# Every tile on chip starts 32 bytes past a multiple of 128: a helper that fills each tensor's row

## The chip, the cores and the metric

The kernel runs on one core of one Trainium2 chip. The metric is device time of one execution, in microseconds, and lower is better.

## The reference, cut to what matters

The reference is one forward pass of three transformer-like blocks over a sequence of 512 positions with 1024 features, everything in float32. What fills the time is dense products of an activation with a weight matrix:

- block 1: a SwiGLU layer (1024 to 2816 and back), a mixer (attention in blocks of 128 keys beside a gated recurrence, two gated projections and an output projection), and a second SwiGLU layer;
- block 2: one wide projection into four mixers (a delta-rule recurrence, gated linear attention, an mLSTM and a state-space mixer), a gated merge, and a feed-forward layer with a causal convolution over three positions on both of its halves;
- block 3: a spatial gating mixer (1024 to 4096 and back), a forgetting attention, and two feed-forward layers (1024 to 2048) whose gate half alone has the convolution.

```python
def swiglu(x, w1, w3, w2):
    return (jax.nn.silu(x @ w1) * (x @ w3)) @ w2
...
def conv_gated_ffn(h, w_gate, w_up, conv_w, conv_b, w_down):
    a = h @ w_gate
    ...                       # causal convolution over 3 positions
    return (jax.nn.silu(a) * (h @ w_up)) @ w_down
```

## The kernel before, in words

**Layout.** Activations lie transposed: a tile `[128, k, 512]` holds feature `k*128 + partition` of all 512 positions. `x` is the residual, `xn` the normalised input of the next product, `hidden` the inner activation of a feed-forward layer.

**A product in three parts.** A float32 value is kept as a pair of rounded values, `hi` and `lo` (type fp32r). Each product of 128 input and 128 output features is three matmuls: (w_hi, x_hi), (w_hi, x_lo) and (w_lo, x_hi). The stationary operand is a slice of 128 columns (512 bytes of a partition's row) of the weight tile, the moving operand 512 columns (2048 bytes) of the activation. Each matmul has a weight load of its own, which the profile shows on a row called PEld. The lines are L280 (`Feed.products`, for the attention and the delta-rule stages), L1108 (`Flow.products`, for the stages named s1 to s4), L1916 (`Side.tensor`, for the stages named hg and br) and L1637, where the roles are turned: there a slice of `xn` is stationary and 512 columns of the weights move.

**How weights come.** SyncE loads a raw slice of 512 KB (128 partitions x 1024 floats), ScalarE rounds it into `w_hi` (L263, L1081, L1928), VectorE subtracts to get `w_lo` (L268, L1088, L1934), and TensorE makes 24 matmuls of it. Two or three slices are held in turn, 4096 bytes apart in a row.

**Stages.** The program is a sequence of blocks, each with its own tiles: s1 (first SwiGLU), att, hg (recurrence, with merge products beside it), s2 (merge, output, second SwiGLU), rw, br (three mixers of block 2 with projections beside them), s3 (merge, output, convolution feed-forward, spatial gating, feed-forward), fox (attention of block 3), s4 (its output and the last feed-forward). In s3 the feed-forward of block 2 has 22 tiles of 128 inner features, and each takes 48 matmuls and an epilogue of ScalarE and VectorE (`ConvGLU`: L1263, L1243, L1267, L1268, L1252, L1274, L1278 to L1280), in whose order the rounding of the next weights (L1081, L1088) is written as well. Each engine's order is written out by hand; engines meet by semaphores.

**Where the tiles lie.** Tiles are given places in a row of SBUF one behind the other as they are opened (an `ExitStack` closes them again), each rounded up to 32 bytes. The first, `table`, starts at byte 16512, a multiple of 128. `column` has 709 floats (2836 bytes, rounded 2848), so what stands behind it, `x`, `xn`, `rs` and the big tiles, starts at 32 modulo 128. All of these have rows that are multiples of 2048 bytes. Small tiles of a stage (`sink`, `gains`, `lbc`, a padded row of 514, 513 or 515 positions) shift the tiles behind them by 32, 64 or 96.

The moving operand of nearly all the dense matmuls starts at 416 modulo 512. The start of the stationary slice, and the distance from the start of the moving to the start of the stationary operand, both modulo 512, are worked out from the shapes:

| weights | stages | stationary modulo 512 | modulo 128 | distance modulo 512 |
|---|---|---|---|---|
| `s_w` in s1 and s2, `side` | s1, s2, hg, br | 416 | 32 | 0 |
| `s_w` in s3 and s4, `hg_w` | s3, s4, hg | 480 | 96 | 64 |
| `att_w` | att | 256 | 0 | 352 |
| `rw_w` | rw | 448 | 64 | 32 |
| `br_w` | br | 384 | 0 | 480 |
| `fox_w` | fox | 96 | 96 | 192 |
| L1637 (`xn` stationary, `s_w` moves) | s3 | 416 | 32 | 448 |

Of the kernel before, what the change touches and what calls it, by code (L numbers as in the profile page):

```python
# [1 line left out]


# [1 line left out]

# [1 line left out]

# [3 lines left out]
F32 = mybir.dt.float32  # L11
# [5 lines left out]
P = 128  # L17
# [77 lines left out]
COLUMN_WIDTH = _at  # L95


class Stage:


# [11 lines left out]
        return self.stack.__exit__(*e)  # L112

    def sb(self, name, shape, dtype=F32):
        return self.stack.enter_context(self.nc.sbuf_tensor(f"{self.name}_{name}", shape, dtype))

    def ps(self, name, shape):
        return self.stack.enter_context(self.nc.psum_tensor(f"{self.name}_{name}", shape, F32))
# [1709 lines left out]
class Sums:  # L1828


    def __init__(self, sb, rs):
        self.total, self.squares, self.sq = sb("total", [P, S]), sb("squares", [P, S]), sb("sq", [P, 2, S])
        self.rs, self.small = rs, sb("small", [P, S])
# [766 lines left out]
def branches(nc, c, a, xn, y_0, y_1, y_2, y_s, part, low, gates, inbox_a, inbox_b, more):  # L2600

    with Stage(nc, "br") as st:
        b = [st.ps(f"b{i}", [P, S]) for i in range(8)]
        side = Side(c, st, [b[6][:, :], b[7][:, :]], 4, more)
        achain, dchain = st.sem("achain"), st.sem("dchain")

        def place(name, make):
            with ExitStack() as s:  # L2610
                return make(lambda n, shape: s.enter_context(nc.sbuf_tensor(f"{name}_{n}", shape, F32)))
        box = [inbox_a[:, m * S:(m + 1) * S] for m in range(4)]
        pad_m = inbox_b[:, 0:2 * (S + 3)].rearrange("p (m t) -> p m t", m=2)
        box_m = [inbox_b[:, 2 * (S + 3) + m * S:2 * (S + 3) + (m + 1) * S] for m in range(2)]
        pad_s = inbox_a[:, 0:3 * (S + 3)].rearrange("p (m t) -> p m t", m=3)
        box_s = inbox_a[:, 3 * (S + 3):3 * (S + 3) + S]
        lanes = Lanes(st, c, low, st.sb, place)
        gla = place("gla", lambda sb: Gla(side, "gla", low[:, 0, :], y_1, sb, box))
        ml = place("ml", lambda sb: Mlstm(side, lanes, "ml", low[:, 0, :], y_2, sb, pad_m, box_m))
        sd = place("sd", lambda sb: Ssd(side, lanes, "sd", low[:, 0, :], y_s, sb, pad_s, box_s))  # L2620
        lanes.scratch(inbox_b[:, 0:3 * S].rearrange("p (n t) -> p n t", n=3), part[:, 0:2, :], part[:, 2, :])
        st.sb("held", [P, 17 * S])
        side.allocate()
        ins = {gla: (a["gla_w"], box), ml: (a["ml_w"], [pad_m[:, 0, 3:], pad_m[:, 1, 3:], *box_m]),
               sd: (a["sd_w"], [pad_s[:, 0, 3:], box_s, pad_s[:, 1, 3:], pad_s[:, 2, 3:]])}
        order = [(branch, h) for branch in (gla, ml, sd) for h in range(4)]
        gla.ask(xn, a["gla_w"][0], box)
        first = len(side.pieces)
        given = {(sd, 0): [0], (sd, 1): [1], (sd, 2): [2], (sd, 3): [3, 4, 5]}
        for n, (branch, h) in enumerate(order):  # L2630


            at = len(side.pieces)
            nth, y = {gla: (0, y_0), ml: (1, y_1), sd: (2, y_2)}[branch]
            if n + 1 < len(order):
                nxt, nh = order[n + 1]
                w_d, outs = ins[nxt]
                nxt.ask(xn, w_d[nh], outs)
            for t in given.get((branch, h), []):
                side.sigmoid(xn, a["mg2_w"][t, 3, :, 0:D], gates[t])  # L2640
            side.gated(xn, y, 4, [(t, a["mg2_w"][t, nth]) for t in (2 * h, 2 * h + 1)], part, part if nth else None)
            branch.beside.append((at, len(side.pieces)))

        with nc.Block() as block:
            @block.sync
            def _(sp):
                gla.sync(sp, a["gla_fup"])
                side.sync(sp)

            @block.tensor  # L2650
            def _(pe):
                lanes.tensor_move(pe, b)
                side.tensor(pe, first * DT)
                lanes.tensor_turn(pe, b)
                lanes.tensor_ends(pe, b)
                gla.tensor(pe, b)
                ml.tensor(pe, b)
                sd.tensor(pe, b)

            @block.scalar  # L2660
            def _(act):
                q = InOrder(act, achain)
                side.scalar_first(act)
                side.scalar(act, 1)
                lanes.scalar(act, q, b)
                side.scalar(act, first - 1)
                gla.scalar(act, q, b)
                ml.scalar(act, q, b, gla)
                sd.scalar(act, q, b)

            @block.vector
            def _(dve):
                q = InOrder(dve, dchain)
                side.vector_first(dve)
                gla.zero(dve)
                side.vector(dve, q, 1)
                lanes.vector(dve, q)
                side.vector(dve, q, first - 1)
                lanes.vector_columns(dve, q, b)
                lanes.vector_decays(dve, q, b)  # L2680
                q(dve.memset(pad_m[:, :, 0:3], 0.0))
                gla.vector(dve, q, b, ml)
                q(dve.memset(pad_s[:, :, 0:3], 0.0))
                ml.vector(dve, q, b, sd)
                sd.vector(dve, q, b)
# [383 lines left out]
def build(nc, a, out_d):  # L3069

    with ExitStack() as keep:
        def sb(name, shape, stack=keep):
            return stack.enter_context(nc.sbuf_tensor(name, shape, F32))

        def pair(name, tiles_, stack):
            return Pair(lambda n, shape, dtype: stack.enter_context(nc.sbuf_tensor(n, shape, dtype)), name, [P, tiles_, S])

        table, column = sb("table", [P, TABLE_WIDTH]), sb("column", [P, COLUMN_WIDTH])

        with ExitStack() as s:  # L3080
            more = [s.enter_context(nc.sbuf_tensor(f"side_{n}", [P, 2, D], F32R)) for n in ("hi", "lo")]
        x, kept = sb("x", [P, DT, S]), nc.dram_tensor("kept", (P, DT, S), F32).ap()
        c = Ctx(nc, table, column)

        with ExitStack() as blocks:
            xn, rs = pair("xn", DT, blocks), sb("rs", [P, S], blocks)

            with ExitStack() as s:
# [221 lines left out]
```

How the kernel before makes its waits and increments, by code:

```python
    def __call__(self, ins):  # L131
        ins.then_inc(self.sem, 1)
        self.n += 1
        self.eng.wait_ge(self.sem, self.base + self.n)
# [14 lines left out]
    def wait(self, eng, name, r=0):  # L149
        eng.wait_ge(self.sem, r * len(self.names) + self.names.index(name) + 1)
# [1 line left out]
    def wait_round(self, eng, r):  # L152
        eng.wait_ge(self.sem, r * len(self.names))
# [75 lines left out]
    def wait(self, eng, k):  # L230
        if self.ready:
            sem, base, step = self.ready
            eng.wait_ge(sem, base + step * (k + 1))
# [17 lines left out]
    def load(self, sp, r, m, first, source):  # L251
        s, slot = self.at(r, m)
        if not first or m >= self.slots:
            sp.wait_ge(self.parted, s - self.slots + 1)
        cols = source.shape[-1]
        sp.dma_start(self.raw[:, slot, 0:cols], source).then_inc(self.landed[slot], 16)
# [1 line left out]
    def round(self, act, r, m, first, cols):  # L258
        s, slot = self.at(r, m)
        act.wait_ge(self.landed[slot], (r * (self.per // self.slots) + m // self.slots + 1) * 16)
        if not first or m >= self.slots:
            act.wait_ge(self.used, s - self.slots + 1)
        act.activation(self.hi[:, slot, 0:cols], self.raw[:, slot, 0:cols], ACT.Copy).then_inc(self.rounded, 1)
# [1 line left out]
    def rest(self, dve, r, m, cols):  # L265
        s, slot = self.at(r, m)
        dve.wait_ge(self.rounded, s + 1)
        dve.tensor_tensor(self.lo[:, slot, 0:cols], self.raw[:, slot, 0:cols], self.hi_value[:, slot, 0:cols],
                          ALU.subtract).then_inc(self.parted, 1)
```

## Time and profile before

| | us |
|---|---|
| median of 3 runs | 4438.67 (4435.94 to 4443.2) |
| the profiled execution, its own time | 4443.0 |
| its span in the trace | 4441.2 |
| TensorE busy | 4021.4 (91%), 18490 matmuls |
| weight loads busy | 3245.4 (73%) |
| VectorE, ScalarE busy | 2139.9 (48%), 1520.6 (34%) |
| granted TensorE clock | 0.955 of full |

Busy time of an engine is the union of its instructions' intervals. Matmuls overlap in the trace (one is shown 390 to 400 ns long while the next starts after some 230), so their mean length is not what one costs: the step from one start to the next is, and it is read from start times, or as busy time over count in a stretch without a gap.

### The profile page before, as it was taken

To read this page: it belongs to the slowest core of one execution; us is meant where nothing else is said; L and a number is where in the kernel's file an instruction comes from. 1 tells how busy PE (TensorE), PEld (TensorE's weight loads), DVE (VectorE), ACT (ScalarE), POOL (GpSimd) and SP (SyncE) were. 2 spreads that over 40 slices of the span, in tenths; PEclk is the share of its full clock that TensorE was granted. 3 is DMA by queue.
4 is the path that set the end of the run, shared out by engine and by line. 5 is a ranking of instruction groups with operands and counts; after the bars stand their busy time and mean duration, and the time that the engine had idled before them with its cause. 6 is when DMAs were issued, how large, how long until landed. Compare 5 with 4: busy or idle time off the path is not lost. (4 is left out here: it accounts for less than half of the span.)

```text
span 4441.2 us, 46915 instructions
## 1 busy us (share of the span) xinstructions
PE 4021.4 (91%) x18490; PEld 3245.4 (73%) x18490; DVE 2139.9 (48%) x3342; ACT 1520.6 (34%) x2330; POOL 0.2 (0%) x4
## 2 busy tenths in 40 slices
PE   9997769998899778877999998999998998887998
PEld 7885658887788667776767776777787886666886
DVE  3334564444533445554445556665346564233563
ACT  2223444443322322224444443333322322444322
POOL 0000000000000000000000000000000000000000
PEclk9998989999999889989999999999998999899999
DMA  4231112222223210102222223233332332110332
GB/s 145 95 97 55 34 43 90 76 81 95 85 96 95 62 37 17 35 1 78 72 67 69 74 69 102 85 88 96 93 104 62 90 96 67 56 43 28 100 95 81
DMA packets 94321, 328.08 MB, mean 74 GB/s; under 512 B 10416, under 2 KB 11440, under 8 KB 93744
## 3 DMA queue, kind: packets, MB, share of 16 engines
q1 hardware_dynamic: 94128, 325.40, 23.6%
q8 instruction: 134, 2.20, 0.2%
q14 instruction: 59, 0.48, 0.0%
HBM read 319.06 MB, written 6.29 MB: 73 GB/s over the span
## 5 line engine op out<-in xcount | busy, mean ns | idle before, releaser
L1088 DVE TENSOR_TENSOR s_w_lo<-s_w_raw,s_w_hi 128x1024 fp32r<-128x1024 f32 (+2 forms) x394 | 471.8, 1198 | 652.3 <-ACT s_w_hi L1081 649.5
L1108 PE MATMUL s_acc<-xn_hi,s_w_hi 128*128 128x512 f32 x1744 | 695.0, 398 | 46.3 <-DVE s_w_lo L1088 18.7
L1108 PE MATMUL s_acc<-xn_lo,s_w_hi 128*128 128x512 f32 x1744 | 689.5, 395 | 0.0
L1108 PE MATMUL s_acc<-xn_hi,s_w_lo 128*128 128x512 f32 x1744 | 688.9, 395 | 0.0
L1081 ACT ACTIVATE s_w_hi<-s_w_raw 128x1024 fp32r<-128x1024 f32 (+2 forms) x394 | 405.5, 1029 | 556.7 <-PE s_acc L1108 442.2
L1108 PEld LDWEIGHTS s_acc<-xn_hi,s_w_hi 128*128 128x128 f32 x1744 | 330.3, 189 | 134.7 <-DVE s_w_lo L1088 26.5
L1108 PEld LDWEIGHTS s_acc<-xn_hi,s_w_lo 128*128 128x128 f32 x1744 | 330.4, 189 | 75.5
L1108 PEld LDWEIGHTS s_acc<-xn_lo,s_w_hi 128*128 128x128 f32 x1744 | 330.6, 190 | 74.8 <-issue 1.2
L1108 PE MATMUL s_acc<-hidden_hi,s_w_hi 128*128 128x512 f32 x784 | 308.0, 393 | 0.7 <-DVE s_w_lo L1088 0.7
L1108 PE MATMUL s_acc<-hidden_lo,s_w_hi 128*128 128x512 f32 x784 | 308.0, 393 | 0.0
L1108 PE MATMUL s_acc<-hidden_hi,s_w_lo 128*128 128x512 f32 x784 | 308.0, 393 | 0.0
L1108 PEld LDWEIGHTS s_acc<-hidden_hi,s_w_hi 128*128 128x128 f32 x784 | 147.4, 188 | 34.2 <-DVE s_w_lo L1088 1.1
L1108 PEld LDWEIGHTS s_acc<-hidden_lo,s_w_hi 128*128 128x128 f32 x784 | 147.4, 188 | 33.3
L1108 PEld LDWEIGHTS s_acc<-hidden_hi,s_w_lo 128*128 128x128 f32 x784 | 147.4, 188 | 33.1
L1916 PE MATMUL br_b<-xn_hi,side_hi 128*128 128x512 f32 x368 | 152.3, 414 | 5.5 <-DVE side_lo L1934 5.5
L1916 PE MATMUL br_b<-xn_hi,side_lo 128*128 128x512 f32 x368 | 144.7, 393 | 0.0
L1916 PE MATMUL br_b<-xn_lo,side_hi 128*128 128x512 f32 x368 | 144.7, 393 | 0.0
L1243 ACT ACTIVATE gate<-pad,column 128x512 f32<-128x512 f32 x54 | 44.1, 817 | 261.9 <-DVE pad L1263 261.9
L1916 PE MATMUL hg_b<-xn_hi,side_hi 128*128 128x512 f32 x256 | 104.8, 409 | 16.6 <-DVE side_lo L1934 10.2
L1916 PE MATMUL br_b<-xn_hi,br_w_hi 128*128 128x512 f32 x256 | 105.6, 412 | 9.5 <-ACT inbox_a L1953 6.8
L1219 DVE SCALAR_TENSOR_TENSOR gate<-gate,s_acc 128x512 f32<-128x512 f32 x44 | 30.3, 689 | 153.1 <-ACT gate L1214 153.1
L1934 DVE TENSOR_TENSOR side_lo<-br_w_raw,side_hi 128x1024 fp32r<-128x1024 f32 (+1 forms) x52 | 60.1, 1162 | 89.4 <-ACT side_hi L1928 89.3
(669 smaller groups left out, 7531.3 us busy)
## 6 DMA issues: line engine op xcount, KB each, us to landing
s_w_raw<-in_f_up SPq DMA_DIRECT2D x132, 512.0 KB, 3.8
s_w_raw<-in_g_up SPq DMA_DIRECT2D x64, 512.0 KB, 3.7
s_w_raw<-in_f_down SPq DMA_DIRECT2D x48, 512.0 KB, 3.5
hg_w_raw<-in_hg_w SPq DMA_DIRECT2D x32, 512.0 KB, 4.1
s_w_raw<-in_g_down SPq DMA_DIRECT2D x32, 512.0 KB, 3.8
br_w_raw<-in_mg_w SPq DMA_DIRECT2D x30, 512.0 KB, 3.6
fox_w_raw<-in_fox_w SPq DMA_DIRECT2D x27, 512.0 KB, 3.6
hg_w_raw<-in_mg_w SPq DMA_DIRECT2D x24, 512.0 KB, 3.8
```

Of the source, the lines that this page charges most:

```text
L1081: act.activation(self.hi[:, s % self.SLOTS, 0:cols], self.raw[:, s % self.RAW, 0:cols], ACT.Copy).then_inc(self.rounded, 1)
L1088: dve.tensor_tensor(self.lo[:, s % self.SLOTS, 0:cols], self.raw[:, s % self.RAW, 0:cols], self.hi_value[:, s % self.SLOTS, 0:cols], ALU.s ...
L1108: last = pe.matmul(out, w[:, slot, tile_cols(k)], v[:, p.k0 + k, :], start=p.start and k == 0 and n == 0, stop=p.stop and k == p.kt - 1 an ...
L1219: q(dve.scalar_tensor_tensor(prod, prod, 0.5, self.acc(t, 1), ALU.mult, ALU.mult))
L1243: act.activation(out[:, i, :], self.pad[:, 2 * i + side, 0:S], ACT.Identity, scale=w(0, t), bias=b(t)).then_inc(self.tapped, 1)
L1916: last = pe.matmul(out, w[slot][:, tile_cols(k)], v[:, k, :], start=k == 0 and n == 0, stop=k == kt - 1 and n == 2)
L1934: dve.tensor_tensor(self.lo[s % self.SLOTS][:, 0:cols], self.raw[:, s % self.RAW, 0:cols], self.hi[s % self.SLOTS][:, 0:cols].bitcast(F32) ...
```

## The change

A helper `room` opens a tile and, behind it, a fill tensor that takes the rest of its row up to a multiple of 128 bytes. All places where the kernel opens small or odd tiles go through it. In front of everything 8 floats (32 bytes) are taken, so that every tile starts at 32 modulo 128. Nothing reads or writes the fill tensors; no instruction is added, removed or moved.

```diff
+LINE = 128
+
+
+def room(nc, stack, name, shape, dtype):
+
+    t = stack.enter_context(nc.sbuf_tensor(name, shape, dtype))
+    fill = -((4 * math.prod(shape[1:]) + 31) // 32 * 32) % LINE // 4
+    if fill:
+        stack.enter_context(nc.sbuf_tensor(f"{name}_fill", [P, fill], dtype))
+    return t
...
     def sb(self, name, shape, dtype=F32):
-        return self.stack.enter_context(self.nc.sbuf_tensor(f"{self.name}_{name}", shape, dtype))
+        return room(self.nc, self.stack, f"{self.name}_{name}", shape, dtype)
...
-                return make(lambda n, shape: s.enter_context(nc.sbuf_tensor(f"{name}_{n}", shape, F32)))
+                return make(lambda n, shape: room(nc, s, f"{name}_{n}", shape, F32))
...
         def sb(name, shape, stack=keep):
-            return stack.enter_context(nc.sbuf_tensor(name, shape, F32))
+            return room(nc, stack, name, shape, F32)
...
+        keep.enter_context(nc.sbuf_tensor("first_fill", [P, 8], F32))
         table, column = sb("table", [P, TABLE_WIDTH]), sb("column", [P, COLUMN_WIDTH])
```

With it the distance from the moving to the stationary operand, modulo 512, is again worked out from the shapes, counted in units of 128 bytes behind `xn`. In s3 and s4 a padded tile of 65 units and `gains` of 1 unit stand before the weights among tiles of whole multiples of 512 bytes: 66 units, so 256. It is 256 in att, hg, br and fox too, and for L1637; 61 units give 128 in rw; it stays 0 in s1, in s2 and for `side`. `table` moves from 0 to 32 modulo 128, the small tiles of rw from 64, those of gla, ml and sd (stage br) from 0, to 32.

## Rows read from the trace of the kernel before

**Rows 1.** The page: busy us of each engine (share of the span), count of instructions.

```profile
PE 4021.4 (91%) x18490; PEld 3245.4 (73%) x18490; DVE 2139.9 (48%) x3342; ACT 1520.6 (34%) x2330; POOL 0.2 (0%) x4
```

**Rows 2.** Windows: us, then busy (count) of PE, PEld, DVE, ACT, POOL; clock, DMA.

```profile
100.00:300.00 200.00, 200.00 (x884) 165.65 (x883) 75.97 (x90) 47.54 (x55) 0.00 (x0) 1.00 0.31 95
3450.00:3650.00 200.00, 200.00 (x858) 160.83 (x857) 117.95 (x151) 63.27 (x76) 0.00 (x0) 1.00 0.31 95
4200.00:4400.00 200.00, 200.00 (x859) 161.32 (x858) 107.90 (x135) 56.07 (x66) 0.00 (x0) 1.00 0.32 95
```

**Rows 3.** Timeline of PE in br (start us, us, instruction): 47, then 48 matmuls.

```profile
2591.28 0.39 PE L1916 MATMUL br_b<-xn_lo,br_w_hi 128*128 128x512 f32 x1
...
2602.00 0.39 PE L1916 MATMUL br_b<-xn_hi,br_w_lo 128*128 128x512 f32 x1
2602.22 0.39 PE L1916 MATMUL br_b<-xn_hi,side_hi 128*128 128x512 f32 x1
...
2612.88 0.40 PE L1916 MATMUL br_b<-xn_hi,side_lo 128*128 128x512 f32 x1
```

**Rows 4.** Timeline of PE: 63 matmuls of fox; 287 of L1637.

```profile
3782.94 0.40 PE L280 MATMUL fox_pj<-xn_hi,fox_w_hi 128*128 128x512 f32 x1
...
3797.14 0.40 PE L280 MATMUL fox_pj<-xn_hi,fox_w_lo 128*128 128x512 f32 x1
3277.88 0.39 PE L1637 MATMUL s_acc<-s_w_hi,xn_lo 128*128 128x512 f32 x1
...
3343.35 0.40 PE L1637 MATMUL s_acc<-s_w_lo,xn_hi 128*128 128x512 f32 x1
```

**Rows 5.** Line L268 on VectorE: ns min/median/max, starts, forms.

```profile
L268 DVE TENSOR_TENSOR fox_w_lo<-fox_w_raw,fox_w_hi x27: 1217/1226/1226, 3777.7 to 4084.1; 128x1024 fp32r<-128x1024 f32 x27
L268 DVE TENSOR_TENSOR att_w_lo<-att_w_raw,att_w_hi x18: 1216/1226/1226, 399.5 to 627.6; 128x1024 fp32r<-128x1024 f32 x18
L268 DVE TENSOR_TENSOR rw_w_lo<-rw_w_raw,rw_w_hi x13: 1215/1217/1226, 1572.1 to 1908.2; 128x1024 fp32r<-128x1024 f32 x13
```

**Rows 6.** Groups by form of PE: count, busy us, mean ns, idle before.

```profile
L746 PE MATMUL rw_b<-low,rw_up 128*128 128x512 f32 x24 | 10.9, 592 | 0.0
L419 PE MATMUL att_sc<-att_box,table 128*128 128x512 f32 x24 | 11.0, 593 | 0.0
L2146 PE MATMUL br_b<-gla_v,gla_kt 128*128 128x128 f32 x56 | 6.9, 275 | 0.0
L2146 PE MATMUL hg_b<-hg_v,hg_kt 128*128 128x128 f32 x112 | 13.8, 275 | 0.0
```

**Rows 7.** Windows of L1108 alone, from s3 to the end, and its 22 tiles.

```profile
2690.00:4441.00 1751.00, 1234.40 (x5208) 981.59 (x5206) 0.97 0.27 81
2785.00:3044.00 259.00, 248.58 (x1049) 195.82 (x1047) 1.00 0.29 85
```

**Rows 8.** Waits: PE from 2850 to 3050, DVE from 2800 to 3040.

```profile
PE s_acc L1108 <- DVE s_w_lo L1088: 10.4, 16, 0.7
DVE s_w_lo L1088 <- ACT s_w_hi L1081: 73.3, 40, 1.8
```

**Rows 9.** Waits of DVE from 3490 to 3650.

```profile
DVE pad L1263 <- PE s_acc L1108: 17.0, 14, 1.3
```

**Rows 10.** Timeline of DVE: the same instruction, one tile later.

```profile
2906.75 0.68 DVE L1263 TENSOR_TENSOR pad<-s_acc,rs 128x512 f32<-128x512 f32 x1
...
2918.88 0.68 DVE L1263 TENSOR_TENSOR pad<-s_acc,rs 128x512 f32<-128x512 f32 x1
```

**Rows 11.** Windows of the tiles hg_w_lo and br_w_lo.

```profile
655.00:1040.00 385.00, 56.94 (x144) 27.06 (x144) 22.02 (x18) 0.98 0.25 77
2015.00:2690.00 675.00, 131.24 (x328) 62.66 (x328) 51.49 (x50) 0.96 0.23 72
```

**Rows 12.** Windows of L280: att and fox.

```profile
395.00:655.00 260.00, 106.13 (x384) 73.29 (x384) 0.90 0.14 44
3770.00:4105.00 335.00, 148.48 (x576) 105.92 (x576) 0.91 0.15 44
```

More of the change, by code:

```diff
@@ L4 @@
 from contextlib import ExitStack
+import math
 import numpy as np
```

## The prediction

> **What bounds the kernel now.** I read the page first. TensorE is busy 91% of the span, VectorE and ScalarE under half [rows 1]; the granted clock is 0.955 of full over the span. (Its weight loads, at 73%, run beside the matmuls.) So the question is not who waits but what one dense matmul costs, and where TensorE is really the bound. In what follows a pace is the time from one matmul's start to the next.
>
> The view by windows answers the first. In a stretch that TensorE fills without a gap, busy time over count is the pace. In s1, from 100 to 300 us, 884 matmuls overlap the 200 us, about two of them cut by the edges: 200/882 is 226.7 ns. The same shape of matmul on the same line in s3 and s4 gives 858 and 859, less one or two for the edges: 200/857 is 233.4 ns [rows 2]. The clock is 1.00 in all three, the DMA share the same. So a late stage pays some 6.7 ns more for each matmul.
>
> The timeline of TensorE in br shows that the stage is not the cause. 47 matmuls with weights from `br_w` go from 2591.28 to 2602.00, 10.72/46 = 233.0 ns each; the next instruction takes its weights from `side`, and 48 of those go from 2602.22 to 2612.88, 10.66/47 = 226.8 ns each [rows 3]. Line, shape, moving operand and bank are the same; the weight tile alone differs. What differs in the tile is where it starts. I take the start addresses of the section on the kernel and set paces beside the distance from moving to stationary operand, modulo 512: distance 0 (s1, `side`) has 226.7; 64 (s3, s4) 233.4; 480 (`br_w`) 233.0; 192 (fox) 14.20/62 = 229.0; and 448 (L1637) 65.47/286 = 228.9 [rows 2 to 4].
>
> That list says two things. First, 32 modulo 128 for a start is not by itself the quantity: L1637's stationary slice starts at 32 modulo 128 and it is not at 226.7, and `fox_w` and s3's weights both start at 96 modulo 128, against the same moving start, with paces of 229.0 and 233.4. So the distance counts, and with a period longer than 128. Second, 192 and 448 are 256 apart and have one pace to 0.1 ns, with opposite roles. I take that for a period of 256: pace is a function of the distance modulo 256.
>
> **The change, part by part.** It adds no instruction, no wait and no transfer; it moves tiles. After it the distance is 256 modulo 512 in att, hg, br, s3, s4 and fox and for L1637, which is 0 modulo 256: by the rule above these paces become 226.7. In rw it becomes 128, a distance of which no row tells; its cost is bounded by the paces seen, 226.7 to 234, against 233 now.
>
> Term 1, the s stages. Line L1108 has 5208 matmuls from 2690 us on [rows 7]. At 233.3 less 226.7, that is 6.67 ns, they are worth 34.7 us if TensorE is the bound everywhere. It is not. In the feed-forward of block 2 (22 tiles, 48 matmuls each, 1056 in all; 1049 fall in the stretch shown [rows 7]) TensorE waits 16 times for 0.65 us on the low part of the weights, while VectorE in the same stretch waits for ScalarE's rounding alone, 73.3 us in 40 waits, and never for TensorE [rows 8]. Two occurrences of L1263 lie 12.13 us apart [rows 10], and 48 matmuls at 233.3 ns take 11.20. So the tile's time is that of a closed ring of VectorE and ScalarE (pad, tap, round, rest, two taps, twice, and the epilogue), with TensorE inside it: faster matmuls only lengthen its waits, from 0.9 to 1.25 us a tile. Those 1056 matmuls are worth nothing (7.0 us off). In the later feed-forward layers, where only one half has the convolution, VectorE does wait for TensorE, 14 times for 1.2 us at the first of its waits in a tile [rows 9]; a tile gets 48 x 6.67 ns = 0.32 us shorter, well inside 1.2, so TensorE stays the bound. Left: 4152 x 6.67 ns = 27.7 us.
>
> Term 2, L1637: 384 matmuls, 228.9 to 226.7, 0.9 us.
>
> Term 3, hg and br: 3 x 144 = 432 matmuls with weights from `hg_w` and 3 x 328 = 984 from `br_w` [rows 11]. 1416 x 6.67 ns = 9.4 us. TensorE fills nearly all of these stages, but recurrences run beside the products; I count 85% of it, 8.0 us, and keep 5 to 11 for the range (a few matmuls at a switch between the two weight tiles are slow now as well).
>
> Term 4, att and fox: 384 and 576 matmuls [rows 12]. For fox 2.3 ns each is 1.3 us. For att I have no run in the rows; with s3's 6.67 ns it is 2.6 us. The softmax chain holds TensorE up in much of both, so half: 2.0 us, bounds 0.5 and 4. rw: 288 matmuls beside chains of VectorE, an unknown distance: taken at nothing, bounds -1 and +2 us.
>
> Edits at nothing. VectorE's weight subtraction has a median of 1226 ns with its tiles at 96 and at 0 modulo 128, and 1217 at 64 [rows 5]: no engine but TensorE shows an address. Plain float32 matmuls of 512 columns have the same mean with both operands at 32 modulo 128 (592) as with one at 32 and `table` at 0 (593), and those of 128 columns 275 ns with tiles at 0 and at 32 [rows 6]. So the move of `table` and of the small tiles is free; from below and above I allow 1 us. What hides it, if ScalarE or VectorE should change by some 10 ns at an instruction, is their idle half; only the ring of the 22 tiles would show it, 22 x 4 x 10 ns = 0.9 us.
>
> Sum: 27.7 + 0.9 + 8.0 + 2.0 = 38.6 us off the profiled execution's 4443.0, that is 4404.4. Its time is 4.3 above the median of the runs; off the median of 4438.7 the forecast is 4400. Its own range: 34 to 45 us off with 3 us of measurement, 4391 to 4408.
>
> **A rule against it.** Rows 3 show two weight tiles, one moving operand and two paces. The Trainium skill, in "SBUF — State Buffer", section "Who interferes with whom", gives TensorE two read ports of its own, one for the moving operand and one for weight loads, independent of each other, and says that it never waits on anyone; then the distance of the two starts could cost nothing, and the sum would be zero. By that rule the time would stay at 4438.7, which is rival B; the trace disagrees with 233.0 against 226.8 ns within 22 us of each other.
>
> **The rivals.**
>
> A. The period is 512 or more, and distance 256 is not like 0. For it: every fast row has distance 0 modulo 512, and I have no row at 256. Against: the one pace of 192 and 448. If 256 runs like 192 does, at 229.0, the s stages give 4152 x 4.33 = 18.0, hg and br 1416 x 4.33 x 0.85 = 5.2, att 0.8: 24 off, 4415. If it runs at 233.3 as 64 does, only L1637 and fox change, both a little slower (384 x 4.4 and half of 576 x 4.3 ns, 2.9 us): 4442, no change to be told.
>
> B. No effect of the distance; paces belong to the weight tile for another reason (its writer, its place far up in the row); the change does then not do what it says, 4438.7. `s_w` of s1 lies in the same part of the row as that of s3 and has the same writer, so 2 in 100.
>
> C. The other side: distance 256 brings the two reads together more than any distance now. One mechanism, in each dense matmul, slower than before from a pace of 233.3 up. The step seen between good and bad is 6.67 ns; one more of it, 240.0, costs 27.7 in s, 384 x 11.1 ns = 4.3 at L1637, 8.0 in hg and br, half of 576 x 11 ns = 3.2 in fox and 1 in att: 44 us, 4483. The ring of the 22 tiles would hide it there still (48 x 240 ns = 11.5 of 12.13 us). Against: the equality of 192 and 448.
>
> D. The VectorE and ScalarE ring takes over in the two later feed-forward layers too, 2 x 16 x 48 = 1536 matmuls, 10.2 us less: 4410. Against: VectorE's waits for TensorE there are four times what a tile loses.
>
> **How the numbers follow.** Forecast (4400): 78 in 100. D (4410): 8. A with a part of the gain (4415): 5. A without gain (4442) and B (4438.7): 4 and 2. C (4483): 3. 0.2% is 9 us, about what can be told from no change here. Faster: 78 + 8 + 5 = 91. Same: 6. Slower: 3. The range reaches below the forecast's own for the case that hg, br and the attentions give all they have (52 us at most with rw and the switches, and 1 us of error: 4386), above to D: 4387 to 4413 leaves out A, B, C and some of the ends.
>
> **What would show it.** In the changed kernel's trace, busy over count in full stretches of s3 and s4 must be 226.7 ns as in s1, and 882 matmuls must fit 200 us; `br_w` and `side` must have one pace; L1637 and fox must fall to 226.7 as well. The 22 tiles must keep 12.13 us each, with TensorE's waits in them grown to some 1.25 us. If s3 stays at 233 and L1637 leaves 228.9, the period is longer than 256 (A); if the 22 tiles get shorter, my ring is wrong; if rw's pace moves, that gives the value at 128. Most dangerous to the forecast is the period, which rests on two rows.

## The result and the profile after

The changed kernel takes 4409.93 us (median of 4 runs, 4401.99 to 4413.45) beside 4439.49 for the kernel before on the same chip: ratio 0.9928 [0.9913, 0.9943], 29.6 us off. On another chip it took 4407.33 (5 runs) beside 4439.71, ratio 0.9927 [0.9914, 0.9941], 32.4 us off. The profiled execution is the lowest of the first four, 4401.99 us, against the profiled 4443.0 of before: 41.0 us. Forecast 4400, range 4387 to 4413: the medians lie inside it, on the upper side.

The page of the changed kernel, busy us of each engine. TensorE has 48.1 us less than in [rows 1] for the same 18490 matmuls and its weight loads 5.8 us less; VectorE and ScalarE have not moved by 2 us.

```profile
PE 3973.3 (90%) x18490; PEld 3239.6 (74%) x18490; DVE 2138.1 (49%) x3342; ACT 1520.7 (35%) x2330; POOL 0.2 (0%) x4
```

Windows of the changed kernel, columns as in [rows 2]: s1, then s3, then s4.

```profile
100.00:300.00 200.00, 200.00 (x884) 165.62 (x883) 75.40 (x90) 47.05 (x55) 0.00 (x0) 1.00 0.30 95
3450.00:3650.00 200.00, 200.00 (x882) 165.22 (x882) 121.69 (x156) 64.85 (x77) 0.00 (x0) 1.00 0.31 95
4150.00:4350.00 200.00, 200.00 (x884) 165.58 (x883) 114.35 (x144) 58.50 (x69) 0.00 (x0) 1.00 0.32 98
```

Where s3 and s4 had 858 and 859 matmuls in 200 us they now have 882 and 884, as s1: one pace, 226.7 ns. The timeline of TensorE in br, the stretch of [rows 3]: 48 matmuls with weights from `br_w` (the first one starts with a longer load) and then 48 from `side`.

```profile
2578.80 0.48 PE L1930 MATMUL br_b<-xn_hi,br_w_hi 128*128 128x512 f32 x1
...
2589.57 0.39 PE L1930 MATMUL br_b<-xn_hi,br_w_lo 128*128 128x512 f32 x1
2589.80 0.39 PE L1930 MATMUL br_b<-xn_hi,side_hi 128*128 128x512 f32 x1
...
2600.45 0.39 PE L1930 MATMUL br_b<-xn_hi,side_lo 128*128 128x512 f32 x1
```

10.77/47 = 229.1 ns with that first start in it (the passes of br that start without one have 226.7), and 10.65/47 = 226.6 for `side`. The step between the two tiles of [rows 3] is gone. The same view for L1651 (L1637 before) and rw, against [rows 4]:

```profile
3257.73 0.39 PE L1651 MATMUL s_acc<-s_w_hi,xn_lo 128*128 128x512 f32 x1
...
3322.60 0.39 PE L1651 MATMUL s_acc<-s_w_lo,xn_hi 128*128 128x512 f32 x1
1697.27 0.80 PE L294 MATMUL rw_b<-xn_hi,rw_w_hi 128*128 128x512 f32 x1
...
1703.01 0.40 PE L294 MATMUL rw_b<-xn_hi,rw_w_lo 128*128 128x512 f32 x1
```

L1651: 64.87/286 = 226.8 ns, 228.9 before. rw, the one stage left at a distance of 128, has 232.3 ns over the gap-free intervals of its passes: the value that no row of before held. (The first of the lines shown is long; from the second, at 1697.90, to the last it is 5.11/22 = 232.3.)

The 22 tiles of block 2's feed-forward: the timeline of VectorE, every second occurrence of L1277 (L1263 before), and the waits of TensorE and of VectorE there, against [rows 8, 10]. (Columns of waits: us in total, times, longest.)

```profile
2893.06 0.68 DVE L1277 TENSOR_TENSOR pad<-s_acc,rs 128x512 f32<-128x512 f32 x1
...
2905.19 0.68 DVE L1277 TENSOR_TENSOR pad<-s_acc,rs 128x512 f32<-128x512 f32 x1
```

```profile
PE s_acc L1122 <- DVE s_w_lo L1102: 15.1, 16, 1.0
```

```profile
DVE s_w_lo L1102 <- ACT s_w_hi L1095: 67.8, 37, 1.8
```

12.13 us a tile, as before. TensorE's wait has gone from 0.65 to 0.94 us, 16 times; VectorE waits for ScalarE alone. From the first of the 44 occurrences to the last it is 259.93 us before and 259.85 now, so what these matmuls gained was waited away again. In the later feed-forward (VectorE's waits, 3460 to 3600 us, against [rows 9]) VectorE still waits for TensorE, so TensorE is the bound there:

```profile
DVE pad L1277 <- PE s_acc L1122: 10.4, 11, 1.0
```

### The profile page after: what moved, and what is told of

It is laid out like the page before. It is cut to its first block and busy times, and to the rows that moved or that the text cites. A ratio compares the mean times of both kernels' runs of the same rounds, so it can differ in the third digit from the quotient of the medians.

```text
span 4400.1 us, 46915 instructions
## 1 busy us (share of the span) xinstructions
PE 3973.3 (90%) x18490; PEld 3239.6 (74%) x18490; DVE 2138.1 (49%) x3342; ACT 1520.7 (35%) x2330; POOL 0.2 (0%) x4
```

## The experiments

Twelve runs (the last is the changed kernel again), in four groups, each group on one chip with its own runs of the kernel before (medians 4440.95, 4439.71, 4438.84 and 4439.27). "Distance" is from the start of the moving to that of the stationary operand, modulo 256. Stages are followed through the profiles from their first matmul to the first of the next.

### Is it the distance, and what is its period?

**map_distances** and **map_distances_2**: the changed kernel, with empty bytes taken before the rounded weights of some stages.

```diff
+SHIFT = {"s1": 96, "s2": 160, "s3": 32, "s4": 64, "att": 128, "hg": 160, "br": 192, "rw": 32, "fox": 480}   # map_distances
+SHIFT = {"s1": 192, "s2": 32, "s3": 128, "s4": 224}                                                       # map_distances_2
+def shift(st):
+    n = SHIFT.get(st.name, 0) // 4
+    if n:
+        st.stack.enter_context(st.nc.sbuf_tensor(f"{st.name}_shift", [P, n], F32))
...
+        shift(st)
         self.hi, self.lo = st.sb("w_hi", [P, slots, cols], F32R), st.sb("w_lo", [P, slots, cols], F32R)
```

> The changed kernel with a block of empty bytes in front of the rounded weights of each stage, so that each stage has another distance from moving to stationary operand. Distances modulo 512 are then 96 in s1, 160 in s2, 288 in s3, 320 in s4, 384 in att, 416 for hg_w, 448 for br_w, 160 in rw, 224 in fox; side and the order of work stay. My theory (pace is a function of the distance modulo 256): s3 runs as rw did before at 32, 233.4 ns; s4 as s3 did before at 64, 233.3; att as rw of the changed kernel at 128, some 232.2; br_w as fox did before at 192, 229.0; fox as br_w did before at 480, 233.3; s1 as att did before at 352, 234.3; rw, s2 and hg_w (160, 160, 416) have one pace of their own between 229 and 235. Rival (period 512 or more): these pairs, 256 apart, have nothing in common, and at least two of s3, s4, br_w and fox miss those paces by more than 1 ns. Rival (period 128): s1 at 96 and fox at 224 run alike, s2 at 160 like s3 at 288, hg_w at 416 too, and rw at 160. Whole time by my theory: 12 us more in s1, some 13 in s2, 28 in s3 and s4, 10 in the rest: about 4465 to 4475.

> The changed kernel with empty bytes before the rounded weights of four stages, other distances than in the first map, each one that another stage has shown: s1 at 192, s2 at 32, s3 at 128, s4 at 224. If the pace belongs to the distance and not to the stage: s1 229.0 ns (as br and fox at 192), s2 233.3 (as rw at 32 before), s3 232.3 (as att and rw at 128), s4 233.4 (as br before and fox at 224). If it belongs to the stage, s1 and s2, which read 234.3 and 233.3 in the first map, come out some other way. 4455 to 4465 us.

4469.51 us and 4452.16 us, one run each (the second below what was expected, 4455 to 4465). Windows of TensorE, the first kernel and then the second: us, busy (count), clock, DMA. In each kernel the four stretches are s1, s2, s3, s4.

```profile
100.00:300.00 200.00, 200.00 (x855) 1.00 0.30 93
1200.00:1400.00 200.00, 200.00 (x859) 1.00 0.29 95
3500.00:3650.00 150.00, 150.00 (x643) 1.00 0.30 93
4190.00:4340.00 150.00, 150.00 (x645) 1.00 0.31 94
```

```profile
100.00:300.00 200.00, 200.00 (x875) 1.00 0.30 95
1200.00:1400.00 200.00, 200.00 (x858) 1.00 0.29 94
3500.00:3650.00 150.00, 150.00 (x647) 1.00 0.31 95
4190.00:4340.00 150.00, 150.00 (x645) 1.00 0.31 95
```

The stage s1, at 884 in the changed kernel, has 855 at 96 and 875 at 192: the stage does not make the pace. Mean interval between starts, over the gap-free runs of matmuls in all traces (L1660 is L1637 in the two map kernels):

| distance modulo 256 | ns | read in |
|---|---|---|
| 0 | 226.7 | all stages |
| 32 | 233.3 | s3, s2; rw before 233.0 |
| 64 | 233.3 | s3 and s4 before, s4 |
| 96 | 234.3 | s1; att before 234.2 |
| 128 | 232.4 | att, rw, s3, L1660 |
| 160 | 233.3 | s2, rw, hg |
| 192 | 228.9, or 233.3 | s1, most of br; L1637 before has both, fox before one or the other by profile |
| 224 | 233.3 | fox, s4, L1660; br before 233.0 |

Except at 192, all stages at one distance agree to some 0.4 ns, and so do the distances that lie 256 apart (0 and 256, 32 and 288, 64 and 320, 96 and 352, 128 and 384, 160 and 416, 224 and 480). The period is 256; rival A and rival C (256 worse than before) are out. The sharp part is that 0 alone is free: the seven other steps of 32 bytes cost 2.2 to 7.6 ns a matmul.

At 192 there are two paces, and the kernel before has both. [rows 4] show the last 287 of L1637's 384 matmuls. The 96 ahead of them, with operands in the same tiles, go at 22.17/95 = 233.4 ns; sixteen small matmuls and one of L1637 lie between:

```profile
3253.46 0.40 PE L1637 MATMUL s_acc<-s_w_hi,xn_hi 128*128 128x512 f32 x1
...
3275.63 0.40 PE L1637 MATMUL s_acc<-s_w_lo,xn_hi 128*128 128x512 f32 x1
3275.86 1.95 PE L1721 MATMUL s_stat<-pad,table 128*128 128x128 f32 x16
```

All four profiles in which this line is at 448 show it so. fox at 192 has 229.0 over the 63 matmuls of [rows 4]; in before_round_first, where fox's tiles lie in the same places, the same stretch has 14.23/61 = 233.3:

```profile
3766.32 0.40 PE L280 MATMUL fox_pj<-xn_lo,fox_w_hi 128*128 128x512 f32 x1
...
3780.55 0.39 PE L280 MATMUL fox_pj<-xn_hi,fox_w_lo 128*128 128x512 f32 x1
```

What picks the pace at 192 stays open. At 0 all 82 gap-free runs of 100 matmuls or more, in ten profiles, have 226.7 to 226.8.

**start_at_0**: the changed kernel without the first 32 bytes.

```diff
-        keep.enter_context(nc.sbuf_tensor("first_fill", [P, 8], F32))
```

> The changed kernel without the 32 bytes that stand first: every tile starts at 0 modulo 128 in place of 32, and every distance between tiles stays. My theory (the distance of the two starts alone counts): 226.7 ns in every stage as in the changed kernel, the time the same within 0.2%, about 4408, ratio to the kernel before 0.993. Rival (the place itself counts, 32 modulo 128 being the good one): dense matmuls in all stages at 229 to 234 ns, 9200 in the s stages alone, so 4440 to 4480, slower than the kernel before.

4402.75 us (5 runs, 4402.46 to 4406.33), ratio 0.9916 [0.9903, 0.993]; all paces stay at 226.7, rw at 232.4. That everything begins at 32 modulo 128 does nothing to the paces (the time is 5 to 7 us below the changed kernel's two medians, which are of other chips); what the change does is to fill the rows, and with that to bring the distances to 0. Rival B's other causes (place in the row, writer of the tile) fall with it and with the maps.

**fine_distances** and **fine_distances_2**: the changed kernel; the weights are read some bytes further on in their tile.

```diff
+def weights(st, name, slots, cols):
+    n = SHIFT.get(st.name, 0) // 4      # s1 4, s2 16, s3 8, s4 252 bytes; in the second s1 16, s2 4, s3 252, s4 8
+    t = st.sb(name, [P, slots * cols + 64], F32R)
+    return t[:, n:n + slots * cols].rearrange("p (s c) -> p s c", s=slots)
```

> The changed kernel with the rounded weights moved by less than 32 bytes inside their tiles: distances modulo 256 of 4 in s1, 16 in s2, 8 in s3 and 252 (4 short of 256) in s4, 0 elsewhere but in rw. If two streams of reads meet in units of some tens of bytes, a shift of 4 or 8 changes nothing (226.7 ns in s1, s3, s4) and 16 little. If the good pace belongs to the exact distance, these run near the 233.3 of 32. I lean to the first at 4, 8 and 252 and expect 226.7 to 230 at 16; whole time then 4405 to 4415, by the rival about 4440 to 4460.

> The changed kernel with the rounded weights read from some bytes further on inside their tile, the four values of the first fine run handed to other stages: s1 16, s2 4, s3 252, s4 8 bytes. In the first run the pace at a fixed distance of 16 (s2) and of 252 (s4) was 233.33 in one gap-free run of matmuls and 226.67 in the next, that at 8 (s3) 230.7 throughout but for L1651's 233.3, that at 4 (s1) 232.4. If a fine distance leaves the matmuls two or more paces between which a gap chooses: s1 (16) and s3 (252) show 226.7 and 233.3 in turns, s2 (4) and s4 (8) something between. If pace is a plain function of distance, also below 32 bytes, s1 reads one value throughout. 4415 to 4445 us.

4438.47 and 4459.06 us, one run each (the second above the 4415 to 4445 expected). My lean, that a few bytes cost nothing, was wrong: 4 bytes cost 5.7 ns (232.4 in s1 and in s2), 8 bytes 4.0 (230.7 in s3 and in s4), 16 bytes 6.7 where they cost. But the pace is no plain function here. The timeline of s2 in the first of the two (16 bytes), around a wait of 1.06 us:

```profile
1179.88 0.39 PE L1129 MATMUL s_acc<-xn_hi,s_w_lo 128*128 128x512 f32 x1
1180.12 0.40 PE L1129 MATMUL s_acc<-xn_hi,s_w_hi 128*128 128x512 f32 x1
1180.35 0.39 PE L1129 MATMUL s_acc<-xn_lo,s_w_hi 128*128 128x512 f32 x1
1180.58 0.40 PE L1129 MATMUL s_acc<-xn_hi,s_w_lo 128*128 128x512 f32 x1
1182.04 0.50 PE L1129 MATMUL s_acc<-xn_hi,s_w_hi 128*128 128x512 f32 x1 [1.06 <-DVE s_w_lo L1109]
1182.38 0.39 PE L1129 MATMUL s_acc<-xn_lo,s_w_hi 128*128 128x512 f32 x1
1182.60 0.39 PE L1129 MATMUL s_acc<-xn_hi,s_w_lo 128*128 128x512 f32 x1
1182.83 0.39 PE L1129 MATMUL s_acc<-xn_hi,s_w_hi 128*128 128x512 f32 x1
```

Windows of TensorE around it, in the same kernel:

```profile
1090.00:1140.00 50.00, 50.00 (x216) 1.00 0.30 101
1190.00:1390.00 200.00, 200.00 (x884) 1.00 0.30 99
```

The 59 matmuls ahead of the wait go at 233.3 ns, the 1511 behind it at 226.7, with operands in the same places. In the second kernel s1, at 16 as well, has 233.3 throughout. At 252 the first kernel's s4 has 226.7 and, behind a gap, 233.3; the second's s3 has 233.3 but for a few short runs, one of them a tile of 48 between two waits (from 2942.6 us, 226.7). L1658 (L1637 before), where the roles are turned, is at 248 in the first kernel and has 233.3; it is at 4 in the second and has 226.7, where s1 and s2 at 4 have 232.4. So there are two paces for at least 4, 16 and 252, as for 192 above, and a stage can change from one to the other at a wait. What picks it stays open.

### What are the terms worth, one by one?

In all three the kernel before is filled in part: `room` fills only the tiles named.

```diff
-    if fill:
+    if fill and name.startswith(WIDE):
+WIDE = ("pad3", "gains3", "pad4", "gains4")                                      # scratch_only
+WIDE = ("hg_", "br_", "gla_", "ml_", "sd_", "inbox_a", "inbox_b")                # branches_only
+WIDE = ("att_", "fox_")                                                          # attention_only
-        keep.enter_context(nc.sbuf_tensor("first_fill", [P, 8], F32))
```

> The kernel before, with only the tiles pad and gains of Scratch (stages s3 and s4) filled up to 128 bytes: it takes the s3 and s4 stages and the 287 matmuls of L1637 to the distance 0 modulo 256 and leaves hg, br, att, rw and fox where they were. My theory: terms 1 and 2 of the prediction alone, 28.6 us of the 38.6, so 4440 - 28.6 = 4411 us (4409 to 4415). The rival that the gain lies in the fill of all tiles (their starts modulo 128, VectorE's and ScalarE's accesses too) expects at most half of the whole, 4425 or more.

> The kernel before, with only the tiles of the stages hg and br (with gla, ml, sd and the two inboxes of br) filled up to 128 bytes: both rounded weights come to distance 0 modulo 256 and nothing else moves. Term 3 of the prediction alone: 8.0 us (5 to 11), so 4440 - 8 = 4432 us, with hg_w and br_w at 226.7 ns instead of 233.3 and 233.0. The run scratch_only measured 4412.95 against 4439.71 and the whole change 4407.33, so terms 3 and 4 together may be worth 5.6 us only; by that this run would read 4434 to 4436. A rival by which hg and br are set by the lanes beside the matmuls expects 4439 to 4441.

> The kernel before, with only the tiles of the two attention stages (att and fox) filled up to 128 bytes, which brings both rounded weights to distance 0 modulo 256. Term 4 of the prediction alone: 2.0 us (0.5 to 4), 4438 against 4440 us. What is open: in the five profiles with att at distance 0 its stage, from its first matmul to the first of the next stage, took 259.8 to 264.5 us (mean 261.0), in the four at 96 it took 264.5 to 265.7 (mean 265.3), which would be 4.3 us and this run 4435.5; fox showed nothing (331.1 against 330.0). The sum of parts says 32.4 - 26.8 - 2.8 = 2.8 us for it, 4437. A stage time of 264 or more here would make the 4.3 us chance.

The pages of scratch_only and of branches_only, busy time:

```profile
PE 3984.4 (90%) x18490; PEld 3243.0 (74%) x18490; DVE 2139.7 (49%) x3342; ACT 1520.3 (34%) x2330; POOL 0.2 (0%) x4
```

```profile
PE 4014.8 (90%) x18490; PEld 3244.7 (73%) x18490; DVE 2139.2 (48%) x3342; ACT 1520.8 (34%) x2330; POOL 0.2 (0%) x4
```

scratch_only: 4412.95 us (5 runs), ratio 0.9941 [0.9928, 0.9955], 26.8 us off where 28.6 were predicted. TensorE's busy time fell by 37.0 and the profiled execution by 32.9 (4443.0 to 4410.15); in the 22 tiles its waits rose from 10.4 to 16.2 us. Two small tiles a stage, in s3 and s4, make five sixths of the whole change's 32.4 us.

branches_only: 4436.02 us (11 runs), ratio 0.9993 [0.9984, 1.0002], 2.8 us off (7 off to 1 on) where 8.0 were predicted. The long gap-free runs of `hg_w` and `br_w` are at 226.7, and TensorE's busy time is 6.6 us less, but the time is not. The lengths of the stages, in the ten profiles other than those of the map and fine kernels (us; for s3 those with the rounding moved, below, are left out):

| stage | distance not 0 | distance 0 |
|---|---|---|
| s3 | 1088.2 to 1089.5 (3 profiles) | 1069.6 to 1071.2 (4) |
| s4 | 331.6 to 333.3 (4) | 322.6 to 323.9 (6) |
| hg | 383.0 to 385.5, mean 384.2 (4) | 380.8 to 383.3, mean 381.8 (6) |
| br | 669.9 to 675.3, mean 672.2 (4) | 669.7 to 673.5, mean 670.6 (6) |
| att | 264.5 to 265.7 (4) | 259.8 to 264.5 (6) |
| fox | 328.6 to 331.7 (4) | 329.7 to 331.6 (6) |

s3 and s4 give 27 us, and their two columns do not overlap. hg gives most of its 2.9 us (432 matmuls), br a fourth of its 6.6 (984), and one stage's profiles differ by as much. br has waits for ScalarE's and VectorE's steps of the recurrences; that the missing part goes there is likely, and no run shows it.

attention_only: 4441.28 us (11 runs, 4431.95 to 4448.43), ratio 1.0007 [0.9998, 1.0016]: no gain to be told, 2.0 us on (1 off to 7 on). Yet its profile shows the att stage at 260.1 us, as four of the five others with att at distance 0 in the table (259.8 to 260.5; one had 264.5), where the four with att at 96 had 264.5 to 265.7. (In map_distances_2 and the two fine kernels, also at 0, it took 264.3, 261.1 and 268.1.) Windows of 401 to 640 us, before, then attention_only, then the changed kernel on the second chip:

```profile
401.00:640.00 239.00, 189.23 (x912) 151.28 (x912) 127.89 (x405) 90.73 (x270) 0.00 (x0) 0.91 0.14 44
```

```profile
401.00:640.00 239.00, 188.56 (x947) 152.17 (x945) 131.46 (x426) 94.64 (x284) 0.00 (x0) 0.93 0.14 44
```

```profile
401.00:640.00 239.00, 188.94 (x924) 152.40 (x923) 128.88 (x411) 91.49 (x273) 0.00 (x0) 0.91 0.14 44
```

The granted clock of the stretch is 0.93 in the shorter one and 0.91 in the two longer ones, of which the second has att at 0 as well; so most of the 4 us of a profile goes with the clock, not with the pace. Over a whole run the same shows: the runs of attention_only at a mean clock of 0.954 took 4439 to 4448 us, those at 0.956 and 0.957 took 4432 to 4436. Whether the distance has a part in that clock is open; the runs leave it a gain of 1 us at most.

### Is the ring what holds the 22 tiles?

ScalarE's rounding of the next weights goes ahead of its tap or Silu in `ConvGLU.scalar`. **round_first** is the changed kernel with it, **before_round_first** the kernel before with it.

```diff
+            self.flow.round(act, s + self.flow.SLOTS)
             if p.bank == 0:
                 self.tap(act, t, 0)
             else:
                 act.wait_ge(self.convolved, t + 1)
                 act.activation(gate, gate, ACT.Silu).then_inc(self.gated, 1)
                 if len(self.taps) > 1:
                     self.tap(act, t, 1)
-            self.flow.round(act, s + self.flow.SLOTS)
```

> The changed kernel with one change of order: in the epilogue of the convolution feed-forward ScalarE rounds the next weights before it makes the first tap, not after it. It tests the claim that the 22 tiles of the feed-forward of block 2 are bound by a closed ring of VectorE and ScalarE (12.13 us a tile with either layout). My theory: VectorE's two waits of 1.83 us a tile for the rounding shrink to some 0.4, the ring falls to about 9.5 us, and TensorE becomes the bound with 48 x 226.7 ns = 10.88 us a tile: 1.25 us x 22 = 27 us off, about 4381. Rival (TensorE or the loads of weights are the bound there in another way): the tiles stay within 0.3 us of 12.13 and the time within 7 us of the changed kernel's.

> The kernel before with the one move of the run round_first (ScalarE rounds the next weights ahead of its tap or Silu in ConvGLU), and no fills: the s stages of block 2 keep their distance of 64 and 233.3 ns a matmul. My theory: the ring of VectorE and ScalarE is what set 12.13 us a tile in the first FFN of block 2, in the kernel before as in the changed one. With the ring shortened the tiles there go by the matmuls, 48 x 233.3 ns = 11.20 us, so 17 to 22 tiles win 0.93 us each: 16 to 20 us, a time of 4420 to 4425 us. Then the distance is worth more once the ring is gone: round_first against this run should be 4423 - 4387 = 36 us, against the 30 us of the changed kernel against the one before. The rival, that the move helps by itself wherever the matmuls are (a shorter wait at every stage's start), expects the same gain here as in round_first, 22 us, and 4418 us or less; one that says the pace of 233.3 was itself the cause of the 12.13 us expects no gain and 4439.

round_first: 4386.64 us, ratio 0.9884 [0.9868, 0.9899]. before_round_first: 4427.18 us, ratio 0.997 [0.9958, 0.9982]. The timeline of VectorE, two occurrences a tile apart, and its waits from 2800 to 3000 us; round_first:

```profile
2882.12 0.69 DVE L1277 TENSOR_TENSOR pad<-s_acc,rs 128x512 f32<-128x512 f32 x1 [1.34 <-PE s_acc L1122]
...
2893.00 0.69 DVE L1277 TENSOR_TENSOR pad<-s_acc,rs 128x512 f32<-128x512 f32 x1 [1.61 <-PE s_acc L1122]
```

```profile
DVE pad L1277 <- PE s_acc L1122: 28.7, 18, 1.6
DVE s_w_lo L1102 <- ACT s_w_hi L1095: 11.6, 37, 0.5
```

and before_round_first:

```profile
2881.16 0.68 DVE L1263 TENSOR_TENSOR pad<-s_acc,rs 128x512 f32<-128x512 f32 x1
...
2892.36 0.68 DVE L1263 TENSOR_TENSOR pad<-s_acc,rs 128x512 f32<-128x512 f32 x1
```

10.88 and 11.20 us a tile: 48 matmuls at 226.7 and at 233.3 ns. TensorE has no wait left there, and VectorE, which never waited for it there, now does 18 times. The ring was the bound at both paces, and one order of three ScalarE instructions made it. In gain both runs fell short of what I had said. In start_at_0 the first five tiles are one gap-free run of 239 matmuls, and only 17 of 22 are spread out by the ring: 17 x 1.25 = 21.2 us, and the two profiles differ by 21.3 (4402.69 and 4381.4), not by 27. The medians differ by less, 16.1 (4402.75 and 4386.64); round_first's profiled execution is the fastest of its four. Without the fills, 16 waits by 0.93 are 14.9, and 12.5 were measured (4427.18 lies above the 4420 to 4425 expected).

**aligned_and_round_first** and, beside it, **after_again**, the changed kernel itself.

```diff
+SHIFT = {"rw": 128}                                                              # 128 bytes before rw's weights
-        keep.enter_context(nc.sbuf_tensor("first_fill", [P, 8], F32))
+            self.flow.round(act, s + self.flow.SLOTS)                            # moved ahead, as above
```

> The changed kernel with three edits: ScalarE's rounding first in ConvGLU, as in round_first; no 32 bytes at the start; and 128 bytes before the rounded weights of stage rw, the one stage that the change left at a distance of 128. My theory: the 32 or so dense matmuls a pass in rw go from 232.3 to 226.7 ns, 1.6 us at most for its 288 matmuls, so 4385 to 4387 us, with 226.7 ns in every stage; no more is to be had from distances. The rival: rw's matmuls are hidden beside its recurrence and it stays at 4387.

> The changed kernel once more, on the chip of the three runs beside it, so that they can be compared with it. 4402 to 4410 us.

4386.91 us (4 runs, 4383.72 to 4396.81), ratio 0.9889 [0.9874, 0.9904], and 4407.33. rw's three longest passes went from 232.4 to 226.8 ns (all its gap-free intervals from 232.3 to 228.8), and the time stayed where round_first was; the stage rw took 440.6 us beside 440.5, so its products do not set its length. With the ring gone the distances are worth 4427.18 - 4386.91 = 40.3 us, with it 4439.71 - 4407.33 = 32.4. The 7.9 between them fit the 1056 matmuls of the 22 tiles, 7.0 by the pace. Both kernels with the rounding first beat the changed kernel's 4407.33 by some 20 us.

## Why the prediction was right, and where it was off

- **The pace belongs to the distance, with a period of 256.** The period is right, and it was the step that carried the rest; the two maps and start_at_0 bear it out. But the evidence for it was lucky: the one pace of 192 and 448 was read from 287 of L1637's 384 matmuls, and the 96 ahead of them have 233.4 in the same trace; fox's 63 have 233.3 in two other profiles of the same places. Pace is thus not a plain function of the distance, as the prediction had it: 192 allows two. The forecast needed only that 256 is like 0, and that held. The Trainium skill's sentence that TensorE's two reads are independent ("SBUF — State Buffer", "Who interferes with whom") would have had 4438.7; the map kernels, in which only places move, disagree with it: s1 went from 226.7 to 234.3 ns a matmul.
- **Term 1 and 2, 28.6 us.** Measured 26.8 (20 to 32) by scratch_only. The exception inside it, 1056 matmuls worth nothing, holds: 12.13 us a tile before and after, and the 7.9 us that appear once the ring is gone. So does the refusal of rival D, whose 4410 is what the first median reads: with it terms 1 and 2 would have been 18.4, outside that interval, and VectorE still waits for TensorE in the later layers. Term 2 was under-sized by some 0.4 us, for the 96 matmuls above. TensorE's wait in the ring was to grow to 1.25 us; the view of waits lists 0.94, 0.3 less than a tile has to spare (12.13 less 10.88), as it listed 0.65 of 0.93 before.
- **Term 3, 8.0 us.** Over-sized. Measured 2.8 (7 off to 1 on). The share of 85% was read from how full TensorE was; by the median a third of these stages' 9.4 us reaches the end, by the stage lengths some 4 us (hg 2.4, br 1.6). What holds the rest back in br is not shown.
- **Term 4, 2.0 us with bounds 0.5 and 4.** Nothing measured (1 off to 7 on). Terms 3 and 4 together are 5.6 us by the difference of scratch_only and the whole change, against 10.0: 4.4 of the 7 to 10 us by which 4400 lies below the medians. The three parts add up to 27.6 of 32.4 us; the runs can't place the other 4.8.
- **rw at nothing** and **the small edits at nothing.** Right: filling rw's distance as well changed no time (its pace at 128 was 232.3 ns), and 0 against 32 modulo 128 changed no pace.
- **The forecast from one execution.** The profiled executions differ by 41.0 us, near 38.6; the medians by 29.6 and 32.4. That nearness is luck. The profile of before lay 4.3 us above its median and that of the changed kernel 7.9 below.

## What to carry to other kernels

Where TensorE runs dense and one pace differs from another for the same shape, set the operands' start addresses side by side before looking at any engine: here 64 bytes, from the row lengths of two small tiles, decided 6.7 ns of 233. Pad small tiles so that the weights and the activation start a multiple of 256 bytes apart, and check by counting matmuls in a full window. A saving on the busiest engine is worth something only where no ring of the others sets the step: find the ring first, since an instruction's place in ScalarE's order was worth half to two thirds of the whole change (16 to 20 us of 32).

## What the runs showed of the hardware

- A dense fp32r matmul of 512 columns, each with its own weight load, starts every 226.7 ns at distance 0 modulo 256, and every 228.9 to 234.3 at the other multiples of 32, at a granted clock of 1.00. At 192 it is 228.9 or 233.3, in one and the same kernel; 64, the same to the other side, has 233.3 alone.
- VectorE, ScalarE and plain float32 matmuls showed no effect of the addresses tried here beyond 1% ([rows 5, 6], and busy times within 2 us on the pages).
- Offsets of 4, 8 and 16 bytes cost 4.0 to 6.7 ns where they cost, and at 4, 16 and 252 there were two paces; at 16 and 252 one stage changed between them at a wait.
- The runs of attention_only spread with the granted clock: 0.957 to 0.954 went with 4432 to 4448 us. The runs of branches_only show it less: the nine at 0.955 took 4432.6 to 4439.7.
